# Layer 2's probabilities and values turned by VectorE in 32x32 blocks and over DRAM, with one-pass index products

## The chip, the cores and the metric

One core of one Trainium2 chip runs the whole program. The metric is the device time in microseconds (us) from the program's start to its end, as the median of several runs. Lower is better.

## The reference, cut to what matters

A two-layer transformer on 512 tokens of width 2048, batch 1. The first layer has three kinds of attention; before one of them an indexer scores all pairs of tokens (16 heads of 64 dimensions) and only the best 128 keys of each query are kept. The second layer has 16 heads with a bias by distance, and 16 heads on an 8x64 grid where a query reads keys near it:

```python
s = jnp.einsum('bhrqd,bhrkd->bhrqk', q_blk, k_blk) * scale + bias_blk
p = jax.nn.softmax(s, axis=-1)
return jnp.einsum('bhrqk,bhrkd->bhrqd', p, v_blk)
```

In the indexer it is `relu(iq @ ik.T)`, weighted and added over the heads. Everything is float32.

## The kernel before, in words

Every large product is made exact enough by splitting both sides in a high and a low part (`w_hi`, `w_lo`; `act_b[0]`, `act_b[1]`) and doing three one-pass products: high by high, low by high, high by low (`rows_t`, recorded at L402, L403 and L404). The weights arrive in chunks of 1 MB through SyncE's queue; ScalarE makes the high part (`split_hi`, L386), VectorE the low part (`split_lo`, L391), and TensorE runs 48 products of 128x512 on a chunk. Two buffers alternate.

Layer 2 is a row of steps 1 to 16 (`pair_step`), one for each pair of heads: 1 to 8 of the first kind ("A2", queries against all 512 keys), 9 to 16 of the grid kind ("N2", "M2" in the code of TensorE, ScalarE and VectorE). In a step TensorE has four chunks (cc = 0 to 3) of the projections of the next pair, and between chunks the attention of this pair. A unit is one block of 128 queries with its two heads (cc again, four in a step). For it TensorE makes the logits (`qk2`, L1052), VectorE adds the bias, takes the maximum (`soft2_a`) and later scales by the sum (`soft2_b`, L1751), and ScalarE takes the exponential between (`exp2`). The product with the values needs keys on the partitions, so TensorE turns the probabilities (`turn2`, L1065) and the values (`v_turn`, L1104) into PSUM, ScalarE and VectorE copy them out (L1313, L2321), and `pv2` (L1082) multiplies, in plain float32, into `bank[O_BANK]`; VectorE applies the gate (`gated2`, L2330, L2337). In an A2 step the units go in pairs: logits before the first and third chunk, turning before the second and fourth. In an M2 step all four are done at once, logits before the first chunk and turning before the third.

GpSimd issues its own DMAs in the order of its program, all on one queue: the bias of a later step (`bias_load`, b<-rows_2d or nl<-rows_n), for the grid kind 8 additions of a mask (`window_bias`, L2730), and the store of the gated result (`y_store`). After step 15 TensorE does the last logits, turns and products in between `early_products`, the first parts of the output product (`out_products`, L1230). They need the low parts of the gathered results, `act_b[1]`, which VectorE makes in pieces (`part_lo`, `last_lo`). Then the engines meet at a barrier, GpSimd loads `xw` (the residual), ScalarE scales `xw[1]` and only then, in `rows_out`, splits the next chunk.

In layer 1 `idx_units` (L871) makes the index products, 64 rows deep, of 512, 384 and 256 columns for two heads, in plain float32.

## Time and profile before

| what | value |
|---|---|
| median of 3 runs | 2594.1 us (2593.2 to 2594.85) |
| the profiled execution's own time | 2594.84 us |
| its span | 2593.3 us |
| TensorE busy | 2578.9 us, 99% |
| VectorE busy | 1185.2 us, 46% |
| ScalarE busy | 782.7 us, 30% |
| GpSimd busy | 221.2 us, 9% |
| mean granted TensorE clock | 0.998 of full speed |

The span is what the trace covers; the own time is 1.5 us more. TensorE's records overlap, because a product is recorded until its pipeline is empty; the time that one costs is the distance from its start to the start of the next.

### The profile page before, as it was taken

The numbers are of one execution on the slowest core, as the hardware profiler recorded it, in microseconds if no ns is written. First come the engines' busy times: TensorE is split into PE (matmuls) and PEld (weight loads), VectorE is DVE, ScalarE is ACT, GpSimd is POOL, SyncE is SP. The second block draws the span as 40 slices with busy tenths as digits, with TensorE's granted clock in tenths as the row PEclk, the third lists the DMA queues.
The fourth block names the chain that finished last, engine by engine and source line by source line (L and its number), as shares of the span: only waits on it lengthen the run. The fifth ranks groups of instructions, "written<-read, shape, count | busy, mean of one in ns | idle before, by whom it ended". The sixth has DMA issues, their size and how long they took to land.

```text
span 2593.3 us, 34091 instructions
## 1 busy us (share of the span) xinstructions
PE 2578.9 (99%) x12916; PEld 2122.4 (82%) x12916; DVE 1185.2 (46%) x2072; ACT 782.7 (30%) x1126; POOL 221.2 (9%) x374
## 2 busy tenths in 40 slices
PE   9999999999999999999999999999999999999998
PEld 7788888887778888888888888888888888888886
DVE  5663222223338864455554333444444435445425
ACT  6322212223324432323222222333323323323321
POOL 0111000000011111120000000000001112111000
PEclk9999999999999999999999999999999999999999
DMA  7557333333344444445444434333232223224432
GB/s 267 169 169 199 113 122 122 122 121 118 118 156 144 152 139 144 149 167 203 170 170 146 154 137 119 99 100 108 88 103 93 88 100 102 97 93 151 162 114 98
DMA packets 71120, 349.26 MB, mean 135 GB/s; under 512 B 11846, under 2 KB 11846, under 8 KB 42934
## 3 DMA queue, kind: packets, MB, share of 16 engines
q1 hardware_dynamic: 38712, 241.58, 26.5%
q0 software_dynamic: 32320, 106.46, 12.9%
q8 instruction: 61, 1.00, 0.2%
q14 instruction: 27, 0.22, 0.0%
HBM read 299.04 MB, written 50.45 MB: 135 GB/s over the span
## 4 chain that ended last, share of the span: by engine, by line
PE 99%; DVE 0%; DMA 0%; ACT 0%; issue 0%; SPq 0%; DVEq 0%; ACTq 0%
PE bank L402 28%; PE bank L404 27%; PE bank L403 27%; PE bank L1230 5%; PE bank L1082 2%; PE bank L1300 2%; PE bank L1065 2%; PE bank L1052 1%; PE bank L934 1%; PE bank L906 1%; PE bank L915 1%; PE bank L871 1%; PE bank L1104 0%; PE bank L929 0%; PE bank L901 0%; PE bank L663 0%
## 5 line engine op out<-in xcount | busy, mean ns | idle before, releaser
L391 DVE TENSOR_TENSOR w_lo<-w_raw,w_hi 128x2048 fp32r<-128x2048 f32 x204 | 467.2, 2290 | 516.9 <-ACT w_hi L386 516.9
L402 PE MATMUL bank<-act_a,w_hi 128*128 128x512 f32 (+1 forms) x1672 | 656.6, 393 | 0.2 <-DVE w_lo L391 0.2
L404 PE MATMUL bank<-act_a,w_hi 128*128 128x512 f32 (+1 forms) x1672 | 651.1, 389 | 0.0
L403 PE MATMUL bank<-act_a,w_lo 128*128 128x512 f32 (+1 forms) x1672 | 650.7, 389 | 0.0
L386 ACT ACTIVATE w_hi<-w_raw 128x2048 fp32r<-128x2048 f32 x203 | 388.4, 1913 | 671.1 <-PE bank L404 606.6
L402 PE MATMUL bank<-act_b,w_hi 128*128 128x512 f32 x1280 | 503.1, 393 | 0.6
L404 PE MATMUL bank<-act_b,w_hi 128*128 128x512 f32 x1280 | 498.4, 389 | 0.0
L403 PE MATMUL bank<-act_b,w_lo 128*128 128x512 f32 x1280 | 498.4, 389 | 0.0
L402 PEld LDWEIGHTS bank<-act_a,w_hi 128*128 128x128 f32 (+1 forms) x1672 | 313.5, 188 | 70.7 <-issue 6.5
L404 PEld LDWEIGHTS bank<-act_a,w_hi 128*128 128x128 f32 (+1 forms) x1672 | 313.5, 187 | 66.2
L403 PEld LDWEIGHTS bank<-act_a,w_lo 128*128 128x128 f32 (+1 forms) x1672 | 313.7, 188 | 64.4
L402 PEld LDWEIGHTS bank<-act_b,w_hi 128*128 128x128 f32 x1280 | 240.2, 188 | 54.9 <-issue 6.2
L404 PEld LDWEIGHTS bank<-act_b,w_hi 128*128 128x128 f32 x1280 | 240.3, 188 | 50.8
L403 PEld LDWEIGHTS bank<-act_b,w_lo 128*128 128x128 f32 x1280 | 240.4, 188 | 48.5
L1230 PE MATMUL bank<-w_hi,act_b 128*128 128x512 f32 x384 | 118.9, 391 | 0.0
L1751 DVE TENSOR_SCALAR prob<-prob,rden 128x256 f32<-128x256 f32 (+1 forms) x216 | 96.7, 457 | 6.8
L1230 PEld LDWEIGHTS bank<-w_hi,act_b 128*128 128x128 f32 x384 | 71.6, 188 | 15.0 <-issue 0.3
L1608 ACT ACTIVATE prob<-prob,nmx 128x512 f32<-128x512 f32 (+1 forms) x128 | 77.4, 607 | 13.7 <-DVE nmx L1751 13.0
L1497 ACT ACTIVATE stage<-bank,half_b 128x512 f32<-128x512 f32 x48 | 30.4, 684 | 153.4 <-PE bank L404 153.4
L1230 PE MATMUL bank<-w_lo,act_b 128*128 128x512 f32 x192 | 74.8, 389 | 0.0
L1313 ACT ACTIVATE qkvg<-bank 128x512 fp32r<-128x512 f32 x32 | 17.4, 596 | 149.3 <-PE bank L404 149.3
L2424 DVE COPY qkvg<-bank 128x512 f32<-128x512 f32 x16 | 11.1, 692 | 112.1 <-PE bank L404 112.1
(316 smaller groups left out, 2215.3 us busy)
## 6 DMA issues: line engine op xcount, KB each, us to landing
w_raw<-wst SPq DMA_DIRECT2D x210, 1024.0 KB, 4.9
mix_d<-stage POOLq DMA_DIRECT2D x24, 512.0 KB, 2.9
mixg<-mix_d POOLq DMA_DIRECT2D x8, 1536.0 KB, 6.7
b<-rows_2d POOLq DMA_DIRECT2D x16, 448.0 KB, 8.0
raw_m<-wst SPq DMA_DIRECT2D x4, 1024.0 KB, 13.5
x_raw<-x_t SPq DMA_DIRECT2D x8, 512.0 KB, 14.8
q_d<-stage POOLq DMA_DIRECT2D x8, 512.0 KB, 3.2
g_d<-stage POOLq DMA_DIRECT2D x8, 512.0 KB, 3.2
```

Of the source, the lines that this page charges most:

```text
L386: act.activation(w_hi[s][:], w_raw[s][:], ACT.Copy).then_inc(hi_ready, 1)
L391: dve.tensor_tensor(w_lo[s][:], w_raw[s][:], w_hi[s][:].bitcast(F32), ALU.subtract).then_inc(lo_ready, 1)
L402: pe.matmul(out_ap, l_hi, r_hi, start=start, stop=False)
L403: pe.matmul(out_ap, l_lo, r_hi, start=False, stop=False)
L404: return pe.matmul(out_ap, l_hi, r_lo, start=False, stop=stop)
L1065: last = pe.transpose(turn_bank(kind, cc, e)[:, c], prob[:, 2 * slot + e, c], ident)
L1082: last = pe.matmul(bank[O_BANK][64 * e:64 * e + 64, c * P:(c + 1) * P], v_tok[par][:, vb, 64 * e:64 * e + 64], turned_to(kind, cc, e)[:, a ...
L1230: last = pe.matmul(bank[4 * s + b][:], act_b[l][:, k, b * P:(b + 1) * P], wt(r[c % 2], kt, 0, 2 * GC, 2 * GC), start=(k == 0 and n == 0 an ...
L1300: last = pe.matmul(dst[:], act_b[l][:, k, b * P:(b + 1) * P], wt(r[c], kt, 0, 2 * GC, 2 * GC), start=False, stop=(k == KT - 1 and n == 2), ...
L1497: act.activation(stage[par][:, n, :], bank[n][:], ACT.Tanh, scale=0.5, bias=half_b[:, bass.ds(4 * i + (2 * t0 + 2 * par + n), 1)])\
L1608: act.activation(pr, pr, ACT.Exp, bias=nmx[:, cc, e:e + 1], accum_out=rs[:, cc, e:e + 1]).then_inc(e2_ready, 1)
L1751: return dve.tensor_scalar(dst, src, by, None, ALU.mult)
```

## The change

**Layer 2.** `turn2` and `v_turn` go, with the copies of their results. VectorE writes the probabilities of a unit (A2) or of two units (N2) turned within blocks of 32x32 to `flip` (`flip2`, four of 128x1024 in an A2 step, two in an N2 step). GpSimd stores this to `flip_d` in DRAM and loads it back as `prob2_t`, in pieces of 1 KB, which completes the transposition (`flip_store`, `flip_load`). The copy of the values out of PSUM becomes a transposition in blocks; GpSimd stores them with four DMAs in pieces of 128 bytes (`v_to_tokens`), waits for them, and loads `v_tok_a` or the windows `v_tok_n`. `pv2` now comes one half step (A2) or one step (M2) after its logits and waits for the loads. In both kinds the attention work stands before the first and the third chunk. **Queries and keys.** ScalarE copies the queries twice, high part and raw (`q_raw`), VectorE both parts of the keys. **Index products.** High and low parts and three one-pass products take the place of plain float32. **The end.** The order after step 15 is new, `pv2` of step 16 moves into the first output group, and the residual product stands one chunk later.

```diff
-                    for e in range(2):
-                        half = slice(64 * e, 64 * e + 64)
-                        pe.matmul(bank[2 + 3 * e + j][:, 0:P * (tb + 1)], qb1[par][half, tb * P:(tb + 1) * P],
-                                  ik_t[half, 0:P * (tb + 1)], start=True, stop=True).then_inc(i_psum, 1)
+                    for n, (q, k) in enumerate(((iq_hi, 0), (iq_lo, 0), (iq_hi, 1))):
+                        for e in range(2):
+                            half = slice(64 * e, 64 * e + 64)
+                            ins = pe.matmul(bank[2 + 3 * e + j][:, 0:P * (tb + 1)], q[par][half, tb * P:(tb + 1) * P],
+                                            ik_parts[k][half, 0:P * (tb + 1)], start=(n == 0), stop=(n == 2))
+                            if n == 2:
+                                ins.then_inc(i_psum, 1)
...
-
-                u, n = unit_of(step, cc), 4 if kind == "A2" else 2
-                slot, off = at2(kind, cc)
-                for e in range(2):
-                    pe.wait_ge(p2_ready, 2 * u + (e + 1))
-                    for b in range(n):
-                        c = slice(off + b * P, off + (b + 1) * P)
-                        last = pe.transpose(turn_bank(kind, cc, e)[:, c], prob[:, 2 * slot + e, c], ident)
-                    last.then_inc(t2_ready, 1)
-
...
+                    turned = prob2_t[slot][:].rearrange("p i (e b q) -> p e b i q", e=2, b=4)
+                else:
+                    c, n, v = cc, 2, v_tok_n[par][:, cc]
+                    turned = prob2_t[slot][:].rearrange("p i (e c b q) -> p c e b i q", e=2, c=2, b=2)[:, cc % 2]
+                pe.wait_ge(iq_loaded[slot], PROB2_T0 + flips(kind, step, cc))
                 if cc == 0:
+                    pe.wait_ge(v2_loaded, v2_loads(kind, step))
                     if not (isinstance(step, int) and step == 1):
...
                         last = pe.matmul(bank[O_BANK][64 * e:64 * e + 64, c * P:(c + 1) * P],
-                                         v_tok[par][:, vb, 64 * e:64 * e + 64], turned_to(kind, cc, e)[:, at2(kind, cc)[1] // P + b, :],
...
+                if kind == "A2" and pair:
+                    for cc in range(2):
+                        pv2("A2", step, cc, par)
+                elif before == "A2" and pair == 0:
+                    for cc in range(2, 4):
+                        pv2("A2", step - 1, cc, 1 - par)
+                elif before == "M2":
+                    for cc in (2 * pair, 2 * pair + 1):
+                        pv2("M2", step - 1, cc, 1 - par)
...
             pe.wait_ge(ev_act, evac_act(15, 1))
             pe.wait_ge(ev_dve, evac_dve(15, 1))
+            for cc in range(2, 4):
+                qk2("M2", 16, cc, 1)
             early_products(0, range(4))
-            v_turn("N2", 16, 1, 0)
+            for cc in range(2, 4):
+                pv2("M2", 15, cc, 0)
             early_products(1, range(4))
-            for cc in range(2):
-                turn2("M2", 16, cc)
-            v_turn("N2", 16, 1, 1)
-            for cc in range(2, 4):
-                turn2("M2", 16, cc)
-            for cc in range(4):
-                pv2("M2", 16, cc, 1)
             pe.wait_ge(l2_ready, 128)
...
+                        for cc in range(4):
+                            pv2("M2", 16, cc, 1)
+                    if c == 3 and n_out == 0:
 
                         pe.wait_ge(xr_loaded[s], 80)
...
+            def idx_query_hi(i, par):
+
+                act.wait_ge(iq_loaded[par], 16 * i + 16)
+                copy(iq_hi[par][:], qb1[par][:]).then_inc(tt_s, 1)
...
-                                    act.wait_ge(x1_out[s], 80)
-                            copy(qkvg[1 - par][1][:], bank[1][:], scale=HD2 ** -0.5)
                             dst, src = q_rows(new, qkvg[1 - par][0][:], bank[0][:])
+                            copy(dst, src)
+                            dst, src = q_rows(new, q_raw[new == "N2"][:], bank[0][:])
...
+            def flip2(kind, step, cc):
+
+                slot = at2(kind, cc)[0]
+                if not (isinstance(step, int) and step == 1 and cc < 2):
+                    dve.wait_ge(flip_stored[slot], flips(kind, step, cc) - 16)
+                src = prob[:, 2 * slot:2 * slot + 2, :]
+                if kind == "A2":
+                    dve.wait_ge(p2_ready, 2 * unit_of(step, cc) + 2)
+                    dve.nop(nofuse=True)
+                    dve.transpose(flip_a[slot][:].rearrange("p j (e m) -> p e j m", e=2),
+                                  src.rearrange("p e (j m) -> p e j m", j=4)).then_inc(flip_ready, 1)
...
+                            dve.tensor_scalar(k_h[:], bank[1][:], HD2 ** -0.5, None, ALU.mult).then_inc(x1h_s, 1)
+                            dve.wait_ge(x1h_s, step + 11)
+                            dve.scalar_tensor_tensor(out=k_l[:], in0=bank[1][:], scalar=HD2 ** -0.5, in1=k_h[:].bitcast(F32),
+                                                     op0=ALU.mult, op1=ALU.subtract).then_inc(ev_dve, 1)
                             dve.wait_ge(ev_act, evac_act(step, 0))
-                            q_l, k_l = qk_lo(new, 1 - par)
...
-                                dve.wait_ge(vw_ready, step - 9)
-                            dve.tensor_copy(qkvg[1 - par][2][:], bank[in2_banks(kind, cc)[0]][:])
...
+                                dve.wait_ge(v2_stored, 64 * step - 64)
+                                dve.nop(nofuse=True)
+                            dst, src = qkvg[1 - par][2][:], bank[in2_banks(kind, cc)[0]][:]
+                            if new == "N2":
+                                dst, src = dst.rearrange("p (w r c) -> p w r c", w=2, r=8), src.rearrange("p (r w c) -> p w r c", w=2, r=8)
...
-            for cc in range(2):
+            for cc in range(4):
                 soft2_b("M2", 16, cc)
+                if cc % 2:
+                    flip2("M2", 16, cc)
+            part_lo(PARTS_2, 1, len(PARTS_1))
             gated2("M2", 15, 0)
-            for cc in range(2, 4):
-                soft2_b("M2", 16, cc)
             last_lo(14, 0, 3)
-            turned2_dve("M2", 16, 1)
-            turned2_dve("M2", 16, 3)
             part_lo(PARTS_2, 3, len(PARTS_1))
+            part_lo(PARTS_2, 4, len(PARTS_1))
+            split_lo(dve, 2 * G_OUT2 + 2, 0)
             gated2("M2", 16, 1)
-            part_lo(PARTS_2, 4, len(PARTS_1))
             last_lo(15, 1, 6)
...
+            def v_to_tokens(kind, step, par):
 
                 pool.wait_ge(ev_dve, evac_dve(step - 1, 1))
+                if not (isinstance(step, int) and step == 1):
+                    pool.wait_ge(v2_loaded, v2_loads("A2" if isinstance(step, int) and step == 9 else kind, step - 1))
                 pool.nop(nofuse=True)
-                for cb in range(4):
-                    last = pool.tensor_copy(v_win[par][:, 256 * cb:256 * cb + 256].rearrange("p (r c) -> p r c", c=32),
-                                            qkvg[par][2][:].rearrange("p (r c) -> p r c", c=64)[:, :, BLK_START[cb]:BLK_START[cb] + 32])
-                last.then_inc(vw_ready, 1)
+                for i in range(4):
+                    pool.dma_start(bass.AP(v2_d, 32 * i, [[16 * P, 32], [P, 16], [1, 32]]),
+                                   qkvg[par][2][32 * i:32 * i + 32, :].rearrange("p (j b) -> p j b", b=32)).then_inc(v2_stored, 16)
+                pool.wait_ge(v2_stored, 64 * step)
+                if not (isinstance(step, int) and step < 3):
+                    pool.wait_ge(pv2_ready, pv2_done(step - 2, 1))
+                pool.nop(nofuse=True)
...
+            def flip_store(kind, step, cc):
+
+                slot = at2(kind, cc)[0]
+                pool.wait_ge(flip_ready, unit_of(step, cc) + (1 if kind == "A2" else 2 - cc % 2))
+                pool.wait_ge(iq_loaded[slot], PROB2_T0 - 16 + flips(kind, step, cc))
+                pool.nop(nofuse=True)
+                pool.dma_start(flip_d[slot].ap(), (flip_a if kind == "A2" else flip_n)[slot][:]).then_inc(flip_stored[slot], 16)
+
...
+            def flip_load(kind, step, cc):
+
+                slot = at2(kind, cc)[0]
+                pool.wait_ge(flip_stored[slot], flips(kind, step, cc))
+                if kind == "A2" and not (isinstance(step, int) and step == 1 and cc < 2):
+                    pool.wait_ge(pv2_ready, pv2_done(step, cc // 2 - 1))
+                elif kind == "N2":
+                    pool.wait_ge(pv2_ready, pv2_done(8, 1) if isinstance(step, int) and step == 9 else pv2_done(step - 1, slot))
+                pool.nop(nofuse=True)
+                pool.dma_start(prob2_t[slot][:], bass.AP(flip_d[slot], 0, [[256, P], [32 * 1024, 4], [1, 256]])).then_inc(iq_loaded[slot], 16)
...
+                if kind:
+                    flips_over(kind, step, 0)
+                if before == "A2":
+                    y_store(step - 1, 1 - par)
+                if kind:
+                    flips_over(kind, step, 1)
+                if before == "N2":
                     y_store(step - 1, 1 - par)
```

On TensorE in the loop of A2 steps, at the border from the first to the second chunk, this stood before (bank<-con,prob are the turns of `turn2`):

```order
L404 MATMUL bank<-act_b_58,w_hi_51 128x512
L1065 MATMUL bank<-con,prob 128x128 [waits prob2_ready]
L1065 MATMUL bank<-con,prob 128x128 x3
L1065 MATMUL bank<-con,prob 128x128 [waits prob2_ready]
L1065 MATMUL bank<-con,prob 128x128 x3
L1065 MATMUL bank<-con,prob 128x128 [waits prob2_ready]
L1065 MATMUL bank<-con,prob 128x128 x3
L1065 MATMUL bank<-con,prob 128x128 [waits prob2_ready]
L1065 MATMUL bank<-con,prob 128x128 x3
L402 MATMUL bank<-act_b_57,w_hi_52 128x512 [waits lo_ready,hi_ready]
```

and this stands there now:

```order
L412 MATMUL bank<-act_b_57,w_hi_51 128x512
L413 MATMUL bank<-act_b_57,w_lo_53 128x512
L414 MATMUL bank<-act_b_58,w_hi_51 128x512
L404 REGISTER_ALU
L412 MATMUL bank<-act_b_57,w_hi_52 128x512 [waits lo_ready,hi_ready]
L413 MATMUL bank<-act_b_57,w_lo_54 128x512
```

The eight rows of turning, 16 transpositions in all, are gone, and nothing takes their place there.

On GpSimd the loop's second A2 step issued this before (b is a bias, y_d the result):

```order
L2717 ISA [waits logits2_ready]
L2717 DMA b_2_127<-rows_2d 128x1x896
L2717 ISA
L2717 DMA b_3_128<-rows_2d 128x1x896
L2747 ISA [waits o2_ready]
L2747 DMA y_d<-o_st_157 128x512
```

and now it issues this from the step's start up to the first store of turned probabilities (v_d is `v2_d`):

```order
L2649 DMA v_d<-qkvg_119 512x1x32 [waits v2_loaded]
L2649 DMA v_d<-qkvg_119 512x1x32 x3
L2651 REGISTER_ALU
L2656 DMA v_tok_a_145<-v_d 128x512 [waits v2_stored,pv2_psum]
L2701 ISA
L2625 ISA [waits logits2_ready]
L2625 DMA b_2_137<-rows_2d 128x1x896
L2625 ISA
L2625 DMA b_3_138<-rows_2d 128x1x896
L2665 ISA
L2666 ISA [waits prob2_flipped]
L2668 DMA flip_d<-flip 128x1024 [waits iq_and_prob2_t_loaded0]
```

The bias loads now stand behind the values' four stores and their load (v_tok_a), and the pair's probabilities stand behind the bias. Another store and the two loads of `prob2_t` follow.

On VectorE, after the last step, this stood between the two halves of `soft2_a` (ISA prob,mx; act_b_58<-o_raw is the `part_lo` of rows 4 to 7):

```order
L1751 TENSOR_SCALAR nmx<-mx 128x1 [waits logits2_ready] x2
L391 TENSOR_TENSOR w_lo_54<-w_raw_50,w_hi_52 128x2048 [waits hi_ready]
L2222 TENSOR_TENSOR act_b_58<-o_raw,act_b_57 128x2048 [waits o_hi]
L2297 ISA prob,mx<-bank,nb_133 128x256 [waits logits2_psum]
L2297 ISA mx 128x1
L2297 ISA prob,mx<-bank,nb_134 128x256 [waits logits2_psum]
```

and this stands right ahead of the same `part_lo` now (the last of the rows):

```order
L2235 RECIPROCAL rden<-rs 128x1 [waits exp2_ready]
L1657 TENSOR_SCALAR prob<-prob,rden 128x256 [waits scale2_chain]
L2235 RECIPROCAL rden<-rs 128x1 [waits exp2_ready]
L1657 TENSOR_SCALAR prob<-prob,rden 128x256 [waits scale2_chain]
L2253 STREAM_TRANSPOSE flip_n_151<-prob 128x4x4x64 [waits prob2_flipped_stored1,prob2_ready]
L2144 TENSOR_TENSOR act_b_58<-o_raw,act_b_57 128x2048 [waits o_hi]
```

That `part_lo` moved behind the second half of `soft2_a`, all eight pieces of `soft2_b` and both block transpositions.

## Rows read from the trace of the kernel before

**Rows 1.** Waits of TensorE over the whole span: total us, times, longest.
```profile
PE bank L402 <- DVE w_lo L1768: 2.1, 1, 2.1
```

**Rows 2.** Timeline, TensorE, A2 step 4: start us, us, operation, count.
```profile
1764.69 0.50 PE L1052 MATMUL bank<-qkvg,qkvg 64*128 64x512 f32 x2
...
1766.29 1.09 PE L1082 MATMUL bank<-prob_t,v_tok 128*64 128x128 f32 x16
...
1768.18 0.50 PE L402 MATMUL bank<-act_b,w_hi 128*128 128x512 f32 x1
...
1779.24 1.91 PE L1065 MATMUL bank<-con,prob 128*128 128x128 f32 x16
...
1781.34 0.48 PE L402 MATMUL bank<-act_b,w_hi 128*128 128x512 f32 x1
...
1792.45 0.50 PE L1052 MATMUL bank<-qkvg,qkvg 64*128 64x512 f32 x2
...
1806.95 1.91 PE L1065 MATMUL bank<-con,prob 128*128 128x128 f32 x16
...
1808.62 0.47 PE L402 MATMUL bank<-act_b,w_hi 128*128 128x512 f32 x1
```

**Rows 3.** Timeline, TensorE, turning in an M2 step.
```profile
2165.76 1.91 PE L1065 MATMUL bank<-con,prob 128*128 128x128 f32 x16
...
2168.62 0.47 PE L402 MATMUL bank<-act_b,w_hi 128*128 128x512 f32 x1
```

**Rows 4.** Timeline, TensorE, one tile of index products.
```profile
591.01 2.21 PE L871 MATMUL bank<-ik_t,qb 64*128 64x512 f32 x12
```

**Rows 5.** Timeline, VectorE, A2 step 4.
```profile
1764.80 0.69 DVE L2424 COPY qkvg<-bank 128x512 f32<-128x512 f32 x1 [8.04 <-PE bank L404]
...
1769.31 2.29 DVE L391 TENSOR_TENSOR w_lo<-w_raw,w_hi 128x2048 fp32r<-128x2048 f32 x1
...
1773.90 0.68 DVE L2330 SCALAR_TENSOR_TENSOR o_st<-bank,qkvg 128x512 f32<-128x512 f32 x1
```

**Rows 6.** DMA issues: KB each, median us from issue to landing.
```profile
b<-rows_2d POOLq DMA_DIRECT2D x16, 448.0 KB, 8.0
...
x_d<-stage POOLq DMA_DIRECT2D x8, 512.0 KB, 2.9
...
nl<-rows_n POOLq DMA_DIRECT2D x16, 256.0 KB, 4.4
...
v_d<-bkv_n POOLq DMA_DIRECT2D x6, 256.0 KB, 4.3
```

**Rows 7.** Groups of GpSimd: busy us, mean ns of one, idle before.
```profile
L2730 POOL TENSOR_TENSOR nb<-nl,con 128x256 f32<-128x256 f32 x64 | 47.1, 771 | 33.0 <-DMA nl<-rows_n 33.0
...
L2531 POOL DMA_DIRECT2D v_d<-bkv_n x6 | 4.5, 1000 | 39.6 <-DVE ckv_n L1751 39.6
```

**Rows 8.** Timeline, TensorE, after the last step.
```profile
2400.90 0.60 PE L1104 MATMUL bank<-con,v_win 128*128 128x128 f32 x4
...
2411.07 0.73 PE L1230 MATMUL bank<-w_hi,act_b 128*128 128x512 f32 x2
```

**Rows 9.** Timeline, VectorE, after the last step.
```profile
2397.12 2.28 DVE L2222 TENSOR_TENSOR act_b<-o_raw,act_b 128x2048 fp32r<-128x2048 f32 x1
...
2402.97 0.88 DVE L2337 SCALAR_TENSOR_TENSOR o_st<-bank,qkvg 128x128 f32<-128x128 f32 x4
...
2405.60 0.69 DVE L2345 TENSOR_TENSOR act_b<-o_st,act_b 128x512 fp32r<-128x512 f32 x1
...
2428.50 2.29 DVE L391 TENSOR_TENSOR w_lo<-w_raw,w_hi 128x2048 fp32r<-128x2048 f32 x1 [7.36 <-ACT w_hi L386]
```

**Rows 10.** Timeline, GpSimd, first load after the barrier.
```profile
2415.53 1.46 POOL L2784 DMA_DIRECT2D xw<-x_d  x2 [20.77 <-DVEq L2463]
```

**Rows 11.** Windows: TensorE, its loads, VectorE, ScalarE, GpSimd busy us; granted clock, DMA share, GB/s.
```profile
8.90:12.30 3.40, 3.38 (x8) 2.64 (x9) 3.40 (x8) 3.40 (x9) 0.00 (x0) 0.53 1.03 381
```

More of the change, by code:

```diff
@@ L1669, in pair_step @@
                         split_hi(act, 2 * g + (cc % 2 + 1), 1 - cc % 2)
[L1670 removed]
+                        if cc % 2 == 0:
+                            for c in (cc, cc + 1):
+                                exp2(kind, step, c)
                     if new:
@@ L2079, in _ @@
                         split_lo(dve, 2 * g + (1 + e), 1 - e)
+                    if not (last and par):
+                        idx_query_lo(t + 1, 1 - par)
+            with dve.Fori(0, 3) as i:
+                idx_dve(i)
+            idx_dve(3, last=True)
             def pick(n_rounds, base):
@@ L2743, in y_store, with flips_over @@
+            def flips_over(kind, step, pair):
+                ccs = (2 * pair, 2 * pair + 1) if kind == "A2" else (2 * pair,)
+                for cc in ccs:
+                    flip_store(kind, step, cc)
+                for cc in ccs:
+                    flip_load(kind, step, cc)
             def y_store(step, par):
@@ L2776, in _ @@
                 pair_step(2 * i + 11, 0, "N2", "N2", "N2")
-            windows(16, 1)
+            v_to_tokens("N2", 16, 1)
+            for pair in range(2):
+                flips_over("N2", 16, pair)
             pool.drain().then_inc(barrier, 1)
```

378 lines of the change are left out of this document (134 added, 244 removed).

## The prediction

> **What bounds the kernel now.** I read the waits first. TensorE waits for another engine once that matters, 2.1 us at the very start [rows 1], and the table shows it busy for 99% of the span: there is no queue, transfer or VectorE time on the path, only TensorE's own row of products. So the trace prices the change by one question, how much TensorE time goes, and by a second, which the trace can't show yet: whether any new wait reaches TensorE. For the first I read TensorE's timeline, start to start. A one-pass product of 512 columns costs 0.227 us (a chunk of 48 takes 10.9). In A2 step 4 the logits begin at 1764.69, the product with the values at 1766.29, the first chunk at 1768.18; at 1779.24 comes the turning, and the next chunk starts 2.10 us later; the second turning takes 1.67 us [rows 2]. I count times in a step from the start of its logits, T.
>
> **What goes from TensorE.** A2: 2.10 + 1.67 = 3.77 us of turning a step [rows 2]. A chunk that follows short products also starts about 0.15 us slower (11.1 us from 1781.34 to 1792.45 against 10.9), and chunks two and four no longer follow any: 4.07 us a step, 8 steps, 32.6 us. M2: the turning takes 2.86 us [rows 3] and its slow start 0.1; against that, the one block of logits and values is cut in two, with three more changes between kinds of product, about 0.4 us. That leaves 2.55 us, 7 steps (9 to 15), 17.9 us. Step 16: from 2400.90 to 2411.07 there are 10.2 us [rows 8], of which 24 wide products are 5.45 and four units of `pv2` 1.9 (the same 16 products as two units of an A2 step, 1768.18 - 1766.29 [rows 2]); 2.8 are turning, 2.5 after the extra breaks. Index products: 2.2 us a tile [rows 4]. The two heads lie in different halves of the rows and run side by side, as the one-pass logits do, so three passes over 512 + 384 + 256 columns are 3 x 1152 / 512 x 0.227 = 1.5 us and a start of 0.1; 8 tiles give about 4 us. Together **57.0 us**.
>
> **What is added and lies beside TensorE.** VectorE: four block transpositions of 1024 columns in an A2 step. No row shows one. Below, a copy from PSUM takes 0.69 us for 512 columns and the low part 2.29 us for 2048 [rows 5], so 1.15 us; above, twice that. I take 1.15, because both rows move about one column per ns. (Vector Engine (DVE) Microarchitecture Reference of the Trainium skill, "The reshape front-end and per-opcode configuration", says that the transposition sustains one element per cycle and lane; no run here shows it yet.) The copies that go were eight of 0.6 us on VectorE and ScalarE, so neither load rises by more than a few per cent, and VectorE is at 46%. Banks 0 and 1 must be empty before the next chunk: values at T+0.1, then the gate product, each 0.69 us [rows 5], done at T+1.5; TensorE has 3.5 us of logits and values until it wants them. In the middle of the step VectorE makes both key parts from PSUM one after the other, 1.5 us, and ScalarE two copies, 1.1 us: also inside 3.5 us. Queries' low part comes later and is wanted 25 us on. The index splits (0.6 us each on ScalarE and VectorE) are made half a group ahead. I cost these at nothing; with that cover gone they would be 0.7 to 1.5 us a step.
>
> **The wait that can appear in an A2 step.** The pair's `pv2` stands behind the next logits: 3.5 + 11.1 + 10.9 + 1.6 gives T+27.1 for the first unit and T+28.0 for the second. By then: softmax ready as now (1773.90 is T+9.2 [rows 5], plus two transpositions), T+10.3 and T+11.5. But GpSimd comes to it last. Its values' stores wait for T+1.5; each has 512 pieces, and the nearest row for 512 pieces is v_d<-bkv_n, 1.0 us of issuing [rows 7] and 4.3 us to landing [rows 6]: the fourth is issued at T+4.6 and lands at T+9. Then `v_tok_a`, then two bias loads of 448 KB, issued by T+10.3, landing in 8.0 us [rows 6], at T+18.3; `flip_store` goes behind them on the same queue and lands at about T+19.3 and T+20.6 (2.9 us alone for 512 KB [rows 6]). The loads have 512 pieces again: 1 us to issue, 4.3 us in all plus the double size, landing at T+24.3 and T+25.8. That is 2.2 us ahead of `pv2`. The second pair of a step has neither values nor bias ahead of it and is early by 6 us. M2 steps have a whole step's time. Below, then, no wait. Above: if the four stores in 128-byte pieces ran one after the other at 4.3 us each, the last would land at T+18.8, 9.8 later, and TensorE would wait 7.6 us in each of 8 steps. The row is nearer to the lower end, for a quarter of the bytes; I take none. Every us of landing beyond T+11.2 costs 8 us in all.
>
> A row and a rule stand against each other here. The row has 512-byte pieces at 4.3 us for 256 KB, hardly behind 2.9 us for 512 KB in long pieces [rows 6]. DMA: Bandwidth & Descriptors of the Trainium skill, "Specifications", puts the least transfer for full rate at 512 bytes, with a read, modify and write below it; the values' pieces are a quarter of that. By the row the sum has no wait; by the rule it would have some part of the third rival below, and no run here has such a piece yet.
>
> In **step 8** GpSimd also makes the first grid bias: nl<-rows_n lands 4.4 us after issue [rows 6], at T+14, and eight additions of 0.77 us [rows 7] end at T+20.3. Stores at T+20.3 and 20.9 land at about T+23.5 and T+24.7, loads at T+28.3 and T+29.5: against T+27.1 and T+28.0 a wait of **1.5 us**.
>
> **The end has two waits.** First: `early_products` on tiles 4 to 7 needs `part_lo`. On VectorE it stood at 2397.12. Now everything that stood between it and 2405.60 comes first, without the gate (0.8 us) and the part itself (2.2 us): 8.48 - 3.0 = 5.5 us [rows 9], and two transpositions, 2.3 us. It starts at 2404.9 and ends at 2407.1 on that clock. TensorE comes to these products at 2400.90 [rows 8] and some 0.2 us of breaks. Wait: **6.0 us**. Behind the `part_lo` are the gate, the other parts and the next low part, all wanted 10 us later.
>
> Second: let P be the end of `pv2` of step 16, which now stands in the first output group. Before, it was 2411.07 and the loads of `xw` were issued at 2415.53 [rows 8, 10], with a 2.2 us part between, which is now ahead of that: the issue comes at P+3.0 (gate 0.8, ScalarE's copy 0.6, low part 0.7, signals). ScalarE must wait for `xw[1]`, scale it and only then split the fourth chunk, whose low part ended at 2428.50 + 2.29 = 2430.8 [rows 9], 15.3 us after the issue: now P+18.3. TensorE wants it after a chunk, 10.9, and the residual products, 32 at the turns' 0.11, 3.5: P+14.4. Wait: **3.9 us**. Before, the issue came ahead of two chunks and the wait was covered.
>
> **The clock.** The granted clock is 1.00 in all but the start. There, after TensorE had waited 2.1 us [rows 1] in a thin stretch, it was 0.53 and eight products started in 3.4 us where 15 would [rows 11]: 1.6 us lost at the 1.2 GHz level. A wait of 6 us may bring that once, one of 3.9 us perhaps: 1.6 + 0.8 = 2.4 us.
>
> **The sum** against the profiled execution's own time: 2594.8 - 57.0 + 1.5 + 6.0 + 3.9 + 2.4 = 2551.6. That execution is 0.7 above the median of the runs, so 2551 us.
>
> **The rivals.**
> - *As above*, within 5 us: 0.54.
> - *No wait at all.* For it: each wait hangs on a cover that misses by 1 to 6 us, and nothing in the trace before waits. Against: the first is 6 us long by plain durations. 2594.1 - 57.0 = 2537; 2537 to 2545 with one of the two waits at the end: 0.13.
> - *The A2 steps wait too*, because the 128-byte pieces are slow, or the weights' transfers of 1 MB, two in that stretch, push the queue of GpSimd. For it: only 2.2 us of margin over five transfers in series. With landing at T+14: 2.8 x 8 = 22 us, 2573. From 2557 to 2589: 0.28.
> - *Slower or no gain.* The same chain, from one more point: the fourth store landing at T+16.6 costs 5.4 us in each of 8 steps and eats all 43 us; at T+18.8, the upper bound, 61 us, 2612. Against: it needs pieces of 128 bytes to cost as much as pieces of 512. Slower: 0.05.
> - *VectorE becomes the bound.* With transpositions at double price it gains some 9 us of work a step of 51; its share stays under 60%, and low parts are made 7 us ahead. The first wait grows by 2.3 us. Inside the first case's range.
>
> **Range and chances.** A measurement of this kernel can tell about 0.2%, 5 us, from no change. Low end 2540, between no wait and one of them; high end 2576, waits of 3 us in each A2 step: about 1 in 10 lies beyond each, less at the low end. The likeliest case's own range is 2546 to 2557. Faster than 2589: 0.92; within 5 us: 0.03; slower: 0.05.
>
> **What would show it.** Right: A2 steps of about 50.7 us from logits to logits (T to T), M2 of 47.7; TensorE without idle time from step 1 to 7; in the waits of TensorE a product L1084 behind a load of prob_t in step 8 alone, an early product behind act_b of about 6 us, and a wide product behind w_lo of about 4 us near the residual products. Wrong: idle time ahead of L1084 in each A2 step, with the landing of the stores from qkvg later than T+11; block transpositions far from 1.15 us; a granted clock below 1 over more than a few us.

## The result, and the profile after the change

The changed kernel takes **2565.8 us** (median of 4 runs, 2564.47 to 2566.76), the kernel before 2593.7 us (median of 4 runs, 2593.2 to 2594.85). The ratio is 0.9893, with a 95% interval of 0.9881 to 0.9905: 27.9 us faster. The forecast was 2551 us in a range of 2540 to 2576. So the sign and the range held, and of the 43 us forecast 28 came; the time lies outside the likeliest case's own range (2546 to 2557). The profiled execution took 2564.47 us, the shortest of its four runs, and the one before 2594.84 us, nearly the longest of its four; that is why the spans below differ by 30.4 us and not by 27.9.

The page of the changed kernel: its span and each engine's busy time.

```profile
span 2562.9 us, 33421 instructions
...
PE 2531.0 (99%) x12484; PEld 2076.8 (81%) x12484; DVE 1216.5 (47%) x2097; ACT 751.5 (29%) x1062; POOL 355.0 (14%) x558
```

TensorE is still at 99%, which says little: 30 us of span went, and both kernels round to the same share. The waits tell more. Waits of TensorE over the span, total us, times, longest (before, the longest was one of 2.1 us at the start [rows 1]; both kernels also wait 1.8 us there for `warm`):

```profile
PE bank L1161 <- DVE act_b L2144: 7.1, 1, 7.1
PE bank L1084 <- DMA prob_t<-flip_d: 6.7, 5, 4.4
PE bank L1161 <- DVE w_lo L401: 2.3, 1, 2.3
...
PE bank L1063 <- DVE qkvg L2336: 1.3, 1, 1.3
```

To see which part of the program gained, I took four marks on TensorE's timeline: the first logits of step 1, of step 9 and of step 16, and the end of the span. In the kernel before:

```profile
1601.58 0.50 PE L1052 MATMUL bank<-qkvg,qkvg 64*128 64x512 f32 x2
...
2039.79 0.39 PE L1052 MATMUL bank<-qkvg,qkvg 64*128 64x256 f32 x2
...
2391.77 0.39 PE L1052 MATMUL bank<-qkvg,qkvg 64*128 64x256 f32 x2
```

In the changed kernel, the same marks (first, sixth and last row) with step 4, step 5 and the two halves of step 8 between them:

```profile
1597.55 0.50 PE L1063 MATMUL bank<-qkvg,qkvg 64*128 64x512 f32 x2
...
1751.02 0.50 PE L1063 MATMUL bank<-qkvg,qkvg 64*128 64x512 f32 x2
...
1802.00 0.50 PE L1063 MATMUL bank<-qkvg,qkvg 64*128 64x512 f32 x2
...
1955.25 0.50 PE L1063 MATMUL bank<-qkvg,qkvg 64*128 64x512 f32 x2
...
1980.76 0.50 PE L1063 MATMUL bank<-qkvg,qkvg 64*128 64x512 f32 x2
...
2014.94 0.39 PE L1063 MATMUL bank<-qkvg,qkvg 64*128 64x256 f32 x2
...
2349.82 0.39 PE L1063 MATMUL bank<-qkvg,qkvg 64*128 64x256 f32 x2
```

A fifth mark splits the stretch ahead of step 1, the first tile of index products. Before it starts at 591.01 [rows 4], and the next chunk at 593.15:

```profile
593.15 0.50 PE L402 MATMUL bank<-act_a,w_hi 128*128 128x512 f32 x1
```

and in the changed kernel:

```profile
589.76 0.50 PE L880 MATMUL bank<-ik_part,iq_hi 64*128 64x512 f32 x2
...
591.54 0.50 PE L412 MATMUL bank<-act_a,w_hi 128*128 128x512 f32 x1
```

| part | before, us | after, us | change | forecast |
|---|---|---|---|---|
| to the first index tile | 591.01 | 589.76 | -1.25 | 0 |
| from there to step 1 | 1010.57 | 1007.79 | -2.8 | -4 |
| steps 1 to 8 (A2) | 438.2 | 417.4 | -20.8 | -32.6 + 1.5 = -31.1 |
| steps 9 to 15 (M2) | 352.0 | 334.9 | -17.1 | -17.9 |
| step 16 to the end | 201.5 | 213.1 | +11.6 | -2.5 + 12.3 = +9.8 |
| span | 2593.3 | 2562.9 | -30.4 | -43.2 |

Only the M2 row is as forecast within 1 us. Up to step 1 the sum of 4.0 us looks as forecast, and that is luck. Of it 1.25 us went before any index product ran: over the first 20 us the granted clock is 1.00 now and was 0.91 in the kernel before, which had the slow products of [rows 11] there. No run shows whether the change or the execution did that. The index products themselves gave 2.8 us: one tile takes 1.78 us from its start to the next chunk, against 2.14.

10.3 of the 12.8 us that are missing went in the A2 steps, though a free one is as short as forecast: from 1751.02 to 1802.00 are 51.0 us (forecast 50.7). Most of the loss sits in one half step: the first half of step 8 takes 1980.76 - 1955.25 = 25.5 us, the second 2014.94 - 1980.76 = 34.2 us. That is 8.7 us, of which 1.5 were forecast.

What happens there is on GpSimd. Its timeline in step 8 (start us, us, idle before, and what ended it):

```profile
1963.13 1.22 POOL L2627 DMA_DIRECT2D nl<-rows_n  x2 [0.45 <-issue]
1971.35 7.69 POOL L2638 TENSOR_TENSOR nb<-nl,con 128x256 f32<-128x256 f32 x8 [6.99 <-DMA nl<-rows_n]
1978.98 0.60 POOL L2668 DMA_DIRECT2D flip_d<-flip  x1
1979.57 0.55 POOL L2668 DMA_DIRECT2D flip_d<-flip_a  x1
1982.55 0.78 POOL L2679 DMA_DIRECT2D prob_t<-flip_d  x1 [2.42 <-DMA flip_d<-flip]
1983.96 0.77 POOL L2679 DMA_DIRECT2D prob_t<-flip_d  x1 [0.64 <-DMA flip_d<-flip_a]
```

The flips' stores have no idle time before them: they were ready and stood behind the mask additions, and these behind 7.0 us of waiting for nl. Of the additions one was long. The additions of step 8, and those of two later rounds, from 2031 and from 2080 (shortest, median and longest, in ns, and the first and last start):

```profile
L2638 POOL TENSOR_TENSOR nb<-nl,con x8: 730/736/2832, 1971.4 to 1978.3; 128x256 f32<-128x256 f32 x8
...
L2638 POOL TENSOR_TENSOR nb<-nl,con x8: 723/728/2851, 2031.0 to 2038.0; 128x256 f32<-128x256 f32 x8
...
L2638 POOL TENSOR_TENSOR nb<-nl,con x8: 722/726/734, 2080.0 to 2084.9; 128x256 f32<-128x256 f32 x8
```

and VectorE in step 8:

```profile
1972.00 2.29 DVE L401 TENSOR_TENSOR w_lo<-w_raw,w_hi 128x2048 fp32r<-128x2048 f32 x1 [4.50 <-ACT w_hi L396]
```

The long addition is the second. It starts at 1972.1, when VectorE has just begun a low part with two inputs in SBUF, and ends 0.6 us after that has ended. The other rounds bear this out: in six of seven the first addition met a running low part, took 1.2 to 2.9 us and ended 0.6 us behind it, the shorter the later it had started. In the one from 2080.0, where the low part (2077.74 to 2080.03) is over, none is long.

TensorE receives the loads at 1986.82 and 1989.54:

```profile
1986.82 1.98 PE L1084 MATMUL bank<-prob_t,v_tok_a 128*64 128x128 f32 x16 [4.40 <-DMA prob_t<-flip_d]
1989.54 1.98 PE L1084 MATMUL bank<-prob_t,v_tok_a 128*64 128x128 f32 x16 [0.74 <-DMA prob_t<-flip_d]
```

16 such products are recorded with 1.09 us elsewhere [rows 2]; here they take 1.98 us. The windows of the changed kernel say why (us, busy of TensorE, its loads, VectorE, ScalarE, GpSimd, then the granted clock): behind the wait in step 8 and behind the first wait at the end the clock was 0.50, the 1.2 GHz level. It fell while TensorE was still idle (in windows of 1 us, 1.00 up to 1984, 0.71, then 0.50) and was back at 1995.

```profile
1985.00:1990.00 5.00, 2.43 (x20) 2.03 (x22) 4.84 (x10) 2.19 (x7) 0.28 (x1) 0.50 0.91 255
1990.00:1995.00 5.00, 5.00 (x25) 3.96 (x22) 2.82 (x6) 0.00 (x0) 1.23 (x2) 0.53 0.81 316
1995.00:2000.00 5.00, 5.00 (x24) 4.12 (x23) 0.00 (x0) 0.00 (x0) 1.53 (x2) 1.00 0.56 181
...
2365.00:2370.00 5.00, 2.10 (x5) 1.75 (x6) 4.23 (x7) 1.42 (x2) 1.32 (x2) 0.50 0.50 129
2370.00:2375.00 5.00, 5.00 (x16) 3.87 (x16) 3.52 (x2) 1.96 (x2) 0.76 (x1) 0.65 0.49 180
```

Of step 8's 8.7 us, 4.40 + 0.74 = 5.1 are idle, so 3.6 are the clock.

At the end, VectorE's timeline shows the part (L2144) for which TensorE waited 7.1 us, right behind the second of the two block transpositions:

```profile
2364.33 1.25 DVE L2253 STREAM_TRANSPOSE flip_n<-prob 128x1024 f32<-128x1024 f32 x1
2365.50 2.25 DVE L2144 TENSOR_TENSOR act_b<-o_raw,act_b 128x2048 fp32r<-128x2048 f32 x1
```

### The profile page after: what moved, and what is told of

The parts are those of the page before. It is cut to its first block, busy times and chain, and to the rows that moved or that the text cites. A ratio compares the mean times of both kernels' runs of the same rounds, so it can differ in the third digit from the quotient of the medians.

```text
span 2562.9 us, 33421 instructions
## 1 busy us (share of the span) xinstructions
PE 2531.0 (99%) x12484; PEld 2076.8 (81%) x12484; DVE 1216.5 (47%) x2097; ACT 751.5 (29%) x1062; POOL 355.0 (14%) x558
## 4 chain that ended last, share of the span: by engine, by line
PE 91%; DMA 4%; DVE 2%; issue 1%; POOL 1%; SPq 1%; ACT 0%; DVEq 0%; POOLq 0%; ACTq 0%
PE bank L412 26%; PE bank L414 26%; PE bank L413 26%; PE bank L1161 5%; PE bank L1236 2%; PE bank L1084 1%; DMA flip_d<-flip 1%; DMA prob_t<-flip_d 1%; PE bank L1063 1%; PE bank L945 1%; PE bank L917 1%; PE bank L926 1%; DMA raw_m<-wst 1%; PE bank L880 1%; DMA flip_d<-flip_a 1%
## 5 line engine op out<-in xcount | busy, mean ns | idle before, releaser
L1657 DVE TENSOR_SCALAR prob<-prob,rden 128x256 f32<-128x256 f32 (+1 forms) x216 | 83.1, 394 | 6.8
L2493 POOL DMA_DIRECT2D mix_d<-stage x24 | 13.2, 551 | 502.7 <-ACT stage L1433 437.7
L1433 ACT ACTIVATE stage<-bank,half_b 128x512 f32<-128x512 f32 x48 | 30.4, 684 | 149.6 <-PE bank L414 149.6
L2649 POOL DMA_DIRECT2D v_d<-qkvg x64 | 41.2, 663 | 213.3 <-DVE qkvg L2336 200.4
## 6 DMA issues: line engine op xcount, KB each, us to landing
b<-rows_2d POOLq DMA_DIRECT2D x16, 448.0 KB, 10.5
```

Source lines behind the costliest of these rows:

```text
L1433: act.activation(stage[par][:, n, :], bank[n][:], ACT.Tanh, scale=0.5, bias=half_b[:, bass.ds(4 * i + (2 * t0 + 2 * par + n), 1)])\
L1657: return dve.tensor_scalar(dst, src, by, None, ALU.mult)
L2649: pool.dma_start(bass.AP(v2_d, 32 * i, [[16 * P, 32], [P, 16], [1, 32]]), qkvg[par][2][32 * i:32 * i + 32, :].rearrange("p (j b) -> p j b" ...
```

## The experiments

All ratios are to 2593.2 to 2593.3 us for the kernel before, on the same chip. The differences from the changed kernel's 2565.8 are between separate sets of runs, in which the kernel before itself differed by up to 0.5 us, and each ratio's interval is 3 to 4 us to either side: differences of 1 to 4 us rest on the traces. The first three start from the changed kernel and move one thing each.

**1. Tiles 4 to 7 first on VectorE.**

```diff
             split_lo(dve, 2 * G_OUT2 + 1, 1)
+            part_lo(PARTS_2, 1, len(PARTS_1))
             for cc in range(2, 4):
                 soft2_a("M2", 16, cc, 1)
...
-            part_lo(PARTS_2, 1, len(PARTS_1))
             gated2("M2", 15, 0)
```

> The changed kernel with the low part of tiles 4 to 7 made by VectorE right after the split of the second output chunk, ahead of the last two units' softmax. Theory: the wait of 7.1 us before the early products of tiles 4 to 7 and the low clock behind it go; the flips of step 16 come 2.2 us later while TensorE reaches their products 7 to 9 us sooner, so 2 to 3 us come back as a wait there: 2559 to 2561 us against 2565.8. Rival 1: nothing comes back, all 7.1 us and some 2.5 us of clock are gained: 2556 to 2557. Rival 2: the residual's load or the weights bind behind it and the gain is under 3 us: 2563 or more.

Measured: 2556.74 us (2555.43 to 2558.4), ratio 0.9857 (0.9842 to 0.9872): 9.1 us less than 2565.8. The wait for act_b is gone, and a new one stands in the timeline before the last products of step 16:

```profile
2380.26 0.98 PE L1084 MATMUL bank<-prob_t,v_tok_n 128*64 128x128 f32 x14 [1.30 <-DMA prob_t<-flip_d]
```

It is 1.3 us, not 2 to 3, and the time lies below the theory's 2559 to 2561, inside rival 1's 2556 to 2557, though rival 1 had nothing come back. The order on VectorE was the cause of the first wait at the end. Its removal gave 9.1 us, more than the 7.1 of the wait, with 1.3 of a new wait already taken off.

**2. Mask additions behind the flips, step 8 only.**

```diff
                     bias_load(following, step + 1, 1 - par)
-                    if following == "N2":
+                    if following == "N2" and kind != "A2":
                         window_bias(step + 1, 1 - par)
...
                 if before == "A2":
                     y_store(step - 1, 1 - par)
+                if following == "N2" and kind == "A2":
+                    window_bias(step + 1, 1 - par)
```

> The changed kernel with the eight mask additions of step 8 put behind the flips of its first two units on GpSimd; nothing else differs. Theory: the additions in front of the flips are the whole cause of step 8's loss, waits and low clock together, 8.7 us: 2556.5 to 2558 us against 2565.8. Rival 1: the two bias loads, which stay in front on the queue, hold the flips as well, and only half goes: 2561 to 2563. Rival 2 (the size forecast for this wait): 1.5 us go, 2564.3.

Measured: 2557.91 us (2557.47 to 2559.72), ratio 0.9866 (0.9851 to 0.9881): 7.9 us less. In its timeline the two products with the values follow the logits at once, and the second half of the step is 2007.33 - 1981.87 = 25.5 us, like any other:

```profile
1981.87 0.50 PE L1063 MATMUL bank<-qkvg,qkvg 64*128 64x512 f32 x2
...
1983.45 1.97 PE L1084 MATMUL bank<-prob_t,v_tok_a 128*64 128x128 f32 x32
...
2007.33 0.39 PE L1063 MATMUL bank<-qkvg,qkvg 64*128 64x256 f32 x2
```

The window's bias work in front of the flips, the wait for nl and the additions, is the whole cause of the 8.7 us. The eight additions, now beside no low part, took 5.58 us instead of 7.69. The small waits of other A2 steps stayed (2.5 us in four) and those steps lost 1 us more than in the changed kernel, which is why the total gained 7.9 and not 8.7.

**3. Bias loads behind the flips in all steps.** `bias_load`, and `window_bias` with it, stand behind `flips_over(kind, step, 0)` and `y_store` on GpSimd.

> The changed kernel with the bias loads (and the mask additions) of every step put behind the flips of its first two units on GpSimd. Theory: the flips' stores no longer queue behind 8 to 10 us of bias transfer, the waits of steps 1 to 3 (1.6 us, with the clock some 2.5) go as well as step 8's 8.7 us: 2554 to 2556 us. Rival 1: the first three steps' waits have another cause (weights' transfers on the same DMA engines), and it ends as with step 8's additions alone, 2557. Rival 2: the biases now come late for the next step's softmax, and steps grow by 1 us or more each: 2565 or more.

Measured: 2553.47 us (2552.45 to 2553.89), ratio 0.9846 (0.9833 to 0.986): 12.3 us less, just below the theory's 2554 to 2556. No wait for flip_d is left, and the eight A2 steps together take 405.9 us (1597.19 to 2003.09) against 417.4: 11.5 us, the 8.7 of step 8 and 2.8 in steps 1, 2, 3 and 6. In steps 1 and 2 these are 1.1 and 1.0 us around the small waits, in steps 3 and 6 0.4 and 0.3 us with no wait listed. The granted clock around the small waits was 1.00, so the low clock that the theory gave them was not there. GpSimd in step 4, of the changed kernel:

```profile
1758.81 1.24 POOL L2625 DMA_DIRECT2D b<-rows_2d  x2 [0.17 <-issue]
1761.13 0.60 POOL L2668 DMA_DIRECT2D flip_d<-flip  x1 [1.07 <-DVE flip L2248]
...
1772.04 0.79 POOL L2679 DMA_DIRECT2D prob_t<-flip_d  x1 [7.92 <-DMA flip_d<-flip]
```

and with the bias behind:

```profile
1758.27 0.63 POOL L2668 DMA_DIRECT2D flip_d<-flip  x1 [2.46 <-DVE flip L2248]
...
1762.71 0.78 POOL L2679 DMA_DIRECT2D prob_t<-flip_d  x1 [1.47 <-DMA flip_d<-flip]
```

From the store's issue to the load's issue it was 10.9 us with two bias transfers ahead on the queue, and is 4.4 us without. The bias now has the rest of the step. So the A2 steps' own small waits came from this order; the weights' transfers, rival 1, were as before and left none.

**4. Index products back in plain float32**, the copies still made. GpSimd's load of the next queries also waits for the tile's products again (one more `wait_ge`, not shown).

```diff
-                    for n, (q, k) in enumerate(((iq_hi, 0), (iq_lo, 0), (iq_hi, 1))):
-                        for e in range(2):
...
+                    for e in range(2):
+                        half = slice(64 * e, 64 * e + 64)
+                        pe.matmul(bank[2 + 3 * e + j][:, 0:P * (tb + 1)], qb1[par][half, tb * P:(tb + 1) * P],
+                                  ik_t[half, 0:P * (tb + 1)], start=True, stop=True).then_inc(i_psum, 1)
```

> The changed kernel with the index products back in plain float32 (the copies of high and low parts are still made, and not used). Theory: the index term is real and alone on TensorE's path, 8 tiles of 0.5 to 0.6 us: 2569.5 to 2570.5 us against 2565.8. Rival: the index products lie under another wait, and the time stays at 2565.8 within 1 us.

Measured: 2568.09 us (2565.12 to 2570.17), ratio 0.9899 (0.9884 to 0.9914). 2.3 us more, less than expected, and within the spread of its runs. The trace is sharper: the first tile starts at 589.91 and step 1 at 1600.51, 1010.6 us as in the kernel before, against 1007.8 with one-pass products. So 2.8 us belong to the index products, not the 4 of the forecast; the timed runs alone would not settle it.

**5 and 6. Filling the idle time.** Work without use on TensorE, in step 8 and at the end, to separate the idle time from the clock. In step 8:

```diff
+                    if isinstance(step, int) and step == 8:
+                        pe.wait_ge(o2_ready, step - 1)
+                        for _ in range(20):
+                            pe.matmul(bank[O_BANK][:], act_b[0][:, 0, 0:P], act_b[0][:, 0, :], start=True, stop=True,
+                                      skip_group_check=True)
                     for cc in range(2):
                         pv2("A2", step, cc, par)
```

> The changed kernel with 20 products of 128x512 whose result is overwritten (4.6 us at full clock) put on TensorE in step 8, between the logits of its last two units and the products that wait for the flips' load; the load lands when it did. It adds work, and the output is the same. Theory: step 8 lost 8.7 us, of which some 5 are the waits themselves and some 4 the low clock that followed the idle time; with the idle time filled the clock stays up and 3 to 4 us come back: 2562 to 2563 us against 2565.8. Rival: the clock falls for another reason (the transfers, or the plain float32 products), and the time stays at 2565 to 2567.

> The changed kernel with 58 products of 128x256 whose result is overwritten (6.7 us at full clock) on TensorE ahead of the last products of step 15, where it otherwise waits 7.1 us for the low part of tiles 4 to 7. Theory: as in step 8, the clock stays up, and 2.5 to 3.5 us come back: 2562.5 to 2563.5 us against 2565.8. Rival: the filling delays what VectorE waits for in turn (the gate of step 15 behind those products), and the time stays or grows: 2566 to 2569.

Measured: 2564.44 us (2563.72 to 2566.35), ratio 0.9891 (0.9876 to 0.9906), and 2563.37 us (2561.88 to 2565.31), ratio 0.9883 (0.9868 to 0.9898). More work, and 1.4 and 2.4 us less time. The first lies between its theory (2562 to 2563) and its rival (2565 to 2567), the second at the upper edge of its theory; both are small against the spread. The windows are clear, of the first:

```profile
1985.00:1990.00 5.00, 4.81 (x33) 3.66 (x31) 4.96 (x15) 3.36 (x9) 1.34 (x3) 1.00 0.77 197
1990.00:1995.00 5.00, 3.69 (x28) 3.07 (x29) 4.30 (x9) 0.00 (x0) 0.69 (x1) 1.00 0.93 321
```

and of the second:

```profile
2365.00:2370.00 5.00, 4.88 (x47) 4.49 (x46) 4.80 (x8) 0.00 (x0) 1.94 (x4) 1.00 0.51 179
2370.00:2375.00 5.00, 5.00 (x24) 4.12 (x23) 3.47 (x5) 3.39 (x3) 1.31 (x2) 1.00 0.63 169
```

The clock stays at 1.00, with the same transfers around it (a DMA share of 0.77 and 0.93 in step 8). So it is TensorE's idle time that brings the low clock. In the profiled executions the second half of step 8 is 31.9 us, 2.2 less than unfilled though the first load was taken 0.4 us after it had landed and the wait for the second was 1.5 us instead of 0.7, and the stretch from the logits of step 16 to its products with the values is 34.4 us against 37.2.

**7. A later issue of the flips.** `y_store` ahead of `flips_over(kind, step, 0)`.

> The changed kernel with the store of the last step's gated result put ahead of the flips on GpSimd in every step that follows an A2 step, so that the flips' first store is issued about 2.5 us later (it has to wait for VectorE's gate). Theory: the flips' landing follows, A2 steps 2 to 8 have no more than 1 us of slack, and each of them waits 1.5 to 2.5 us more, with low clock behind each: 2577 to 2590 us. Rival 1: the stores queue behind the bias transfers on the same queue anyway, so that a later issue is not a later landing, and the time stays at 2566 to 2568. Rival 2: slack is 2 us or more, as forecast: 2566 to 2570.

Measured: 2569.7 us (2567.08 to 2570.53), ratio 0.991 (0.9895 to 0.9925): 3.9 us more, with overlapping intervals. My theory (2577 or more) fell: the sum of the waits for flip_d rose from 6.7 to 9.0 us, not by 10 to 20. In step 2 of this kernel:

```profile
1654.11 1.26 POOL L2625 DMA_DIRECT2D b<-rows_2d  x2 [0.38 <-issue]
...
1660.21 0.56 POOL L2668 DMA_DIRECT2D flip_d<-flip  x1 [0.23 <-issue]
...
1669.37 0.78 POOL L2679 DMA_DIRECT2D prob_t<-flip_d  x1 [7.92 <-DMA flip_d<-flip]
```

From the bias loads' issue to the flips' load it is 15.3 us here. In the same step of the changed kernel it is 13.6 (1655.75 to 1669.33), with the store issued 1.9 us behind the bias and not 6.1. So of 4.2 us of lateness 1.7 were left; the rest vanished behind the bias transfers, as rival 1 has it. The time lies outside rival 1's 2566 to 2568 and inside rival 2's 2566 to 2570, but rival 2's reason, a slack of 2 us or more, isn't borne out: steps 2 to 7 each lost 0.6 to 1.8 us.

**8. Every transposition of the probabilities twice**, on the kernel of experiment 3: one more `dve.transpose` of the same tile ahead of each.

> The kernel with the biases behind the flips (2553.5 us), in which VectorE makes every one of its block transpositions of the probabilities twice, with the same result: 48 more of 1.2 us. Theory: VectorE is off the path in all steps, and the flips have some 9 us of slack in A2 steps; only at the end does VectorE's row set TensorE's wait (the low part of tiles 4 to 7 stands behind two transpositions), so 2.5 us and a little clock are lost there alone: 2556 to 2557 us. Rival 1: VectorE is close to being the bound, for the logits' banks or the split weights, and each step grows by 1 us or more: 2565 or more. Rival 2: nothing shows at all, 2553 to 2554.

Measured: 2555.06 us (2553.45 to 2562.2), ratio 0.986 (0.9845 to 0.9875), 1.6 us more than its base, not clear of the spread by itself. VectorE is busy 58 us longer (1286.0 against 1227.6), and it shows in one place, the wait for act_b, which was 6.8 us in the base:

```profile
PE bank L1162 <- DVE act_b L2145: 9.4, 1, 9.4
```

2.6 us there, two transpositions of 1.246; the A2 steps together take 405.9 us as in the base. The theory has the place and the price of the wait; the total is 1 us under it.

**9 and 10. The orders together.** Experiments 1 and 3, and on ScalarE the split of the fourth output chunk ahead of scaling `xw[1]`, and the last tanh ahead of `y_hi(1)`. The tenth kernel also issues both flip stores of step 16 before the first load.

```diff
-                    if c == 3:
-                        act.wait_ge(xr_loaded[(n_out + 1) % 2], 16 * ((n_out + 1) // 2) + 80)
...
                     if 4 * n_out + c < 13:
                         split_hi(act, 2 * G_OUT2 + 4 * n_out + c, c % 2)
+                    if c == 3:
+                        act.wait_ge(xr_loaded[(n_out + 1) % 2], 16 * ((n_out + 1) // 2) + 80)
...
             for pair in range(2):
-                flips_over("N2", 16, pair)
+                flip_store("N2", 16, 2 * pair)
+            for pair in range(2):
+                flip_load("N2", 16, 2 * pair)
```

> The changed kernel with four orders changed together: biases behind the flips on GpSimd, the low part of tiles 4 to 7 ahead of the last two units' softmax on VectorE, the split of the fourth output chunk ahead of the residual's scaling on ScalarE, and the last tanh ahead of the high part of tiles 4 to 7 on ScalarE. Theory: the gains measured apart add up (12.3 and 9.1 us), and the last two take the waits of 2.3 and 1.3 us away: 2540 to 2542 us. Rival: at the end each wait that goes uncovers the flips of step 16 or the load behind the barrier, and the last two edits give nothing: 2543 to 2545.

> The kernel with the four mended orders and one more: in step 16 GpSimd issues both stores of the flips ahead of the first load, not store, load, store, load. Theory: the second load is issued some 4 us sooner, and the wait of 2.4 us before the products of step 16, with the low clock behind it, goes: 2539 to 2541 us against 2543.2. Rival 1: the products then wait for the first load or for the values' windows just as long, 2543. Rival 2: the wait goes, but the barrier and the residual's load behind it come no sooner and become the next wait: 2542 to 2543.

Measured: 2543.16 us (2540.56 to 2547.23), ratio 0.981 (0.9797 to 0.9823), and **2538.91 us** (2538.46 to 2539.26), ratio 0.979 (0.9777 to 0.9803). The first is above its theory (2540 to 2542) and at its rival. The waits for the gate and for w_lo in the output product are gone, but the flips of step 16 came up as the next one, with the clock behind it, as the rival said:

```profile
2367.62 1.58 PE L1084 MATMUL bank<-prob_t,v_tok_n 128*64 128x128 f32 x16 [2.43 <-DMA prob_t<-flip_d]
...
2366.00:2371.00 5.00, 3.38 (x21) 2.67 (x21) 1.07 (x5) 0.68 (x2) 0.00 (x0) 0.71 0.66 270
```

The second is at the lower edge of its theory. No wait of TensorE from step 1 on is listed, the longest ones being at the start:

```profile
PE bank L700 <- POOL warm L2424: 1.8, 1, 1.8
PE bank L412 <- DVE w_lo L1713: 0.7, 1, 0.7
```

It is 26.9 us faster than the changed kernel and 54.4 us, 2.1%, faster than the kernel before, with as many instructions on every engine as the changed kernel.

## Why the prediction was right in part

- *What goes from TensorE, 57.0 us.* Right within 3 us. Experiment 10 has no wait from step 1 on, and its span is 56.0 us under that of the kernel before, 1.6 of them ahead of the first index tile, for which there was no term. That leaves 54.4: index tiles 2.7 (4), A2 32.3 (32.6, so 4.0 a step), M2 17.1 (17.9, 2.4 a step and not 2.55), step 16 to the end 2.2 (2.5). The index term was mis-sized: the tile fell from 2.14 to 1.78 us, where the forecast had 2.2 to 1.6.
- *What lies beside TensorE.* Right. The block transposition takes 1.246 us, not 1.15, for 1024 columns and 0.72 for 512. Vector Engine (DVE) Microarchitecture Reference of the Trainium skill, "The reshape front-end and per-opcode configuration", says one element per cycle and lane; the trace agrees in that a block transposition is about as fast as a copy of 512 columns, 0.69 [rows 5]. Experiment 8 shows the cover: every transposition made twice costs 2.6 us of wait in one place.
- *The values' stores.* Right, and the worry was empty. The fourth store has landed when `v_tok_a` is issued, in step 4 at 1758.01, T+7.0 (forecast T+9). DMA: Bandwidth & Descriptors, "Specifications" of the Trainium skill, puts short pieces below full rate; with 64 KB a store landing in 2.2 us, that is not seen to matter here.
- *No wait in A2 steps.* Nearly right. The bias lands in 10.5 us (forecast 8.0), the flips' load was issued at T+21.0, and the 2.2 us of margin shrank to about 1 us; three waits of 0.3 to 0.7 us appeared in steps 1 and 2. Against 8 free steps the A2 part lost 11.5 us, of which 8.7 are step 8 and 2.8 steps 1, 2, 3 and 6; experiment 3, with the bias behind the flips, has all 11.5 back. The third rival (each A2 step waits, 2557 to 2589 us) holds the measured time in its range but is not what happened. The range's upper part was there for that rival, so that it held is in part luck.
- *Step 8, 1.5 us.* **This term failed**, 8.7 us. The mechanism was as described, the size was not. The grid bias landed at T+16.1 (forecast T+14), as `nl` took 7.2 us and not 4.4 [rows 6]. The additions took 7.7 us and not 6.2: the second of the eight stood beside VectorE's low part and took 2.8 us, the others 0.73. So the stores went at T+23.7 instead of T+20.3, and the wait was 5.1 us. The forecast had taken a median and a mean over the whole program, for a place where both run beside other work. The clock then took 3.6 us, for which this place had no term.
- *The first wait at the end, 6.0 us.* Right in place and cause, 7.1 us. From the end of the low part of a weight chunk to this one VectorE took 8.6 us, where the forecast had 7.8, in part because transpositions were longer. A wait of 1.3 us for the gate (L1063 behind L2336), not forecast, stands ahead of it.
- *The second, 3.9 us.* Right in place; 2.3 us. The chain from the load's issue to the low part took 13.9 us instead of 15.3.
- *The clock, 2.4 us.* Too low: 3.6 in step 8 and, by the stretches of experiment 6, 2.9 at the end. The second wait at the end, 2.3 us, for which 0.8 were set, cost none: the clock stayed at 1.00. The forecast had scaled one row of the start [rows 11], where the wait was 2.1 us long; behind waits of 5 and 7 us the low clock held for the next 7 and 5 us of work. A clock below 1 over more than a few us was among the prediction's own signs of being wrong, and it came.

Together: step 8 idle 3.6, the clock 4.1, the other A2 losses 2.8, M2 0.8, the index tiles 1.2, the end's waits 0.8, less the 1.25 won at the start, are some 12 of the 12.8 us by which the span missed; the rest is spread.

I did not try each kind of step with and without the transposition, nor the queries' raw copy alone; their terms rest on the timelines.

## What to carry to other kernels

When work leaves a saturated engine for a longer chain, time the chain by what stands ahead of it in each queue's order, in each kind of step, the odd step between two loops most of all. Here moving loads that nobody awaits behind transfers that TensorE awaits gave back 12.3 us, and changes of order at the end most of the rest. Check a part that comes out as forecast with a mark inside it: the 4.0 us up to step 1 were 2.8 of the cause and 1.25 of something else. Price a wait on TensorE with its clock: one of 5 to 7 us cost about 3 to 4 us more than it lasted, and one that is removed can uncover the next, so look for that one before you stop.

## What the runs showed of the hardware

- Waits of 5.1 us (4.4 and 0.7) and 7.1 us left TensorE at a granted clock of 0.50 for the next 7 and 5 us of its work. In the changed kernel one of 2.3 us left it at 1.00 (before 2406.03, both windows around it), while one of 2.4 us in experiment 9 brought 0.71 over the window of 5 us around and behind it. Filled with useless products, the same stretches stayed at 1.00. Idle time is what matters, and its length alone doesn't decide it.
- A 512 KB store took 4.4 us to the next load's issue on a free queue and 10.9 us with two bias transfers of 448 KB issued just ahead on the same queue.
- A GpSimd addition of 128x256 took 1.2 to 2.9 us when it met VectorE's low part of a weight chunk (2.29 us, two inputs in SBUF), in 7 of 8 rounds of the changed kernel, and always ended 0.6 us behind it; the others took 0.73 us. SBUF — State Buffer of the Trainium skill, "SBUF: two separate sides", says that such a VectorE operation and a GpSimd one that reads SBUF exclude each other for a whole instruction. The trace agrees: the addition waited, and the low part kept its 2.29 us.
